# x's halves and the operands of ff2 and w_pe start at another byte within 512 bytes of SBUF

## What is computed

```python
h = rmsnorm(x, norm1_g[i]);  z = h @ w_in[i] + b_in[i]        # 1024 -> 12296 columns
# mLSTM over mq, mk, mv, mo and retention over rq, rk, rv, rg, both chunkwise
merged = sigmoid(gm) * (y_m @ w_bm[i]) + sigmoid(gr) * (y_r @ w_br[i])
x = x + merged @ w_out[i]
h2 = rmsnorm(x, norm2_g[i])
x = x + square(relu(h2 @ w_ff1[i] + b_ff1[i])) @ w_ff2[i] + b_ff2[i]   # 1024 -> 4096 -> 1024
h3 = rmsnorm(x, norm3_g[i])
x = x + sigmoid(h3 @ w_pe_gate[i]) * (p[i] @ w_pe[i])
```

## The kernel before

| buffer | first byte | modulo 512 |
|---|---|---|
| `raw` / `w_lo` | 2176 | 128 |
| `w_hi` | 34944 | 128 |
| `x_hi_lo`: hi half, alias `free_a` | 59520 | 128 |
| `x_hi_lo`: lo half, alias `free_b` | 75904 | 128 |
| `xn` | 108672 | 128 |
| `BIG` / `BIGR` | 179072 | 384 |

## Time and profile before

### The profile page before, as it was taken

How to read it: one execution, slowest core, us unless ns; L and a number is a source line. 1 busy time by engine, 2 the same in 40 slices (tenths; PEclk the granted TensorE clock), 3 DMA queues, 4 the chain that set the end, 5 groups by cost and what they waited for, 6 DMA issues and landing times.

```text
span 2379.8 us, 32080 instructions
## 1 busy us (share of the span) xinstructions
PE 2292.7 (96%) x13686; PEld 1954.9 (82%) x13686; DVE 1496.3 (63%) x1893; ACT 1028.4 (43%) x1256; POOL 0.2 (0%) x4
## 2 busy tenths in 40 slices
PE   6998989999998999999999999999999999999997
PEld 3775667777786878888998878999989987789997
DVE  4777543333346576765877767666678767767475
ACT  4255441121225265544663435444555534435343
POOL 0000000000000000000000000000000000000000
PEclk9999989999998999999999999999999999999999
DMA  8530034444422252555555544454555545345552
GB/s 329 206 148 1 36 126 193 159 195 159 159 106 107 88 125 89 195 188 205 215 185 178 184 171 160 178 191 178 179 188 196 187 176 198 141 178 183 177 183 101
DMA packets 61397, 389.12 MB, mean 164 GB/s; under 512 B 6600, under 2 KB 11080, under 8 KB 16072
## 3 DMA queue, kind: packets, MB, share of 16 engines
q1 hardware_dynamic: 61256, 387.08, 44.7%
HBM read 386.01 MB, written 1.05 MB: 163 GB/s over the span
## 4 chain that ended last, share of the span: by engine, by line
PE 86%; DVE 7%; ACT 4%; issue 2%; DMA 1%; SPq 0%; DVEq 0%; ACTq 0%
PE PS L509 23%; PE PS L511 23%; PE PS L510 23%; PE PS L615 5%; PE PS L613 3%; PE PS L864 1%; DMA raw<-chunks_in 1%; PE PS L1041 1%; DVE w_lo L1722 1%; ACT w_hi L1244 1%; ACT xn L1322 1%; PE PS L743 1%; PE PS L1023 1%; PE PS L703 1%; PE PS L768 1%
## 5 line engine op out<-in xcount | busy, mean ns | idle before, releaser
L1722 DVE TENSOR_TENSOR w_lo<-raw,w_hi 128x2048 fp32r<-128x2048 f32 x300 | 683.4, 2290 | 492.7 <-ACT w_hi L1244 491.6
L1244 ACT ACTIVATE w_hi<-raw 128x2048 fp32r<-128x2048 f32 x300 | 571.6, 1912 | 696.8 <-PE PS L511 323.8
L509 PE MATMUL PS<-x_hi_lo,w_hi 128*128 128x256 f32 (+1 forms) x1760 | 546.2, 310 | 9.7 <-DVE x_hi_lo L1787 5.2
L511 PE MATMUL PS<-x_hi_lo,w_lo 128*128 128x256 f32 (+1 forms) x1760 | 543.4, 309 | 0.0
L510 PE MATMUL PS<-x_hi_lo,w_hi 128*128 128x256 f32 (+1 forms) x1696 | 518.6, 306 | 0.0
L509 PEld LDWEIGHTS PS<-x_hi_lo,w_hi 128*128 128x128 f32 x1760 | 337.1, 192 | 36.3 <-issue 19.6
L511 PEld LDWEIGHTS PS<-x_hi_lo,w_lo 128*128 128x128 f32 x1760 | 337.0, 191 | 16.8
L510 PEld LDWEIGHTS PS<-x_hi_lo,w_hi 128*128 128x128 f32 x1696 | 325.1, 192 | 14.0
L509 PE MATMUL PS<-w_hi,x_hi_lo 128*128 128x512 f32 (+1 forms) x800 | 317.9, 397 | 15.6 <-DVE x_hi_lo L1787 10.8
L510 PE MATMUL PS<-w_lo,x_hi_lo 128*128 128x512 f32 (+1 forms) x800 | 313.5, 392 | 0.0
L511 PE MATMUL PS<-w_hi,x_hi_lo 128*128 128x512 f32 (+1 forms) x800 | 313.5, 392 | 0.0
(11 more groups left out here) (326 smaller groups left out, 2666.1 us busy)
## 6 DMA issues: line engine op xcount, KB each, us to landing
raw<-chunks_in SPq DMA_DIRECT2D x348, 1024.0 KB, 4.8
bias_ring<-brows_in SPq DMA_DIRECT2D x32, 256.0 KB, 5.0
G<-nrows_in SPq DMA_DIRECT2D x2, 1536.0 KB, 6.7
BIG<-rel_in SPq DMA_DIRECT2D x4, 512.0 KB, 7.7
free_b<-rel_in SPq DMA_DIRECT2D x4, 512.0 KB, 7.8
tabt<-tabs_in SPq DMA_DIRECT2D x1, 1536.0 KB, 11.7
X<-x_in SPq DMA_DIRECT2D x1, 1024.0 KB, 8.5
X<-ctx_in SPq DMA_DIRECT2D x1, 1024.0 KB, 10.5
```

Of the source, the lines that this page charges most:

```text
L509: pe.matmul(o, lhs[0], rhs[0], start=start, stop=False, **more)
L511: return pe.matmul(o, lhs[1], rhs[0], start=False, stop=stop, **more)
L1244: act.activation(w_hi[:, i % HI_RING, :], ring[:, n % RING, :], ACT.Copy).then_inc(*hi_ready.now(n))
L1722: dve.tensor_tensor(w_lo[:, c % RING, :], ring[:, c % RING, :], w_hi[:, i % HI_RING, :].bitcast(F32), ALU.subtract).then_inc(*lo_ready.now(c))
```

## The change

The halves of `x_hi_lo` grow from 4096 to 4224 floats (`X_HALF`), and every view of them that the second block uses starts 112 floats (448 bytes) into its half (`X_AT`). Counted from the arena's start, such an operand begins 64 bytes short of a multiple of 512. `ff2T`, `pT2` and `pw` start 48 floats later in BIG (`FF_AT`), which comes to the same place. Everything placed behind x moves up by 1024 bytes. `x_both` keeps its shape and takes the new start; the views of the first block's wider matmuls (`hT[4]`, `y4T`) and its layer 1 output projection (`yT_na`), `ff_both` and w_bm's and w_br's operands stay where they are modulo 512.

In absolute bytes of the partition, as built:

| operand | before, modulo 512 | after, modulo 512 |
|---|---|---|
| x hi and lo, 256 tokens | 128 | 64 |
| ff2T, pT2 | 384 | 64 |
| w_hi, w_lo | 128 | 128 |

```diff
+X_HALF = 4096 + 128
+X_AT = 112
+FF_AT = 48
...
-        xboth_, xhi_at = place("x_hi_lo", 8192, F32R)
-        xhi_, xlo_, xlo_at = xboth_[:, 0:4096], xboth_[:, 4096:8192], xhi_at + 4096
-        free_a, _ = place("free_a", 4096, F32, xhi_at)
-        free_b, _ = place("free_b", 4096, F32, xlo_at)
+        xboth_, xhi_at = place("x_hi_lo", 2 * X_HALF, F32R)
+        xhi_, xlo_, xlo_at = xboth_[:, 0:X_HALF], xboth_[:, X_HALF:2 * X_HALF], xhi_at + X_HALF
+        free_a, _ = place("free_a", X_HALF, F32, xhi_at)
+        free_b, _ = place("free_b", X_HALF, F32, xlo_at)
...
-        hT = {4: pair_of((xhi_, xlo_), 512, KD), 2: pair_of((xhi_, xlo_), 256, KD)}
-        hT_b = pair_of((xhi_[:, 2048:4096], xlo_[:, 2048:4096]), 256, KD)
+        hT = {4: pair_of((xhi_, xlo_), 512, KD), 2: pair_of((xhi_[:, X_AT:], xlo_[:, X_AT:]), 256, KD)}
+        hT_b = pair_of((xhi_[:, X_AT + 2048:], xlo_[:, X_AT + 2048:]), 256, KD)
...
-        mv = free_a[:, 2048:4096].rearrange("p (t c) -> p t c", t=2)
-        mo = free_b[:, 2048:4096].rearrange("p (t c) -> p t c", t=2)
+        mv = free_a[:, X_AT + 2048:X_AT + 4096].rearrange("p (t c) -> p t c", t=2)
+        mo = free_b[:, X_AT + 2048:X_AT + 4096].rearrange("p (t c) -> p t c", t=2)
...
-        hr = [free_a[:, 2048:4096], free_b[:, 2048:4096]]
+        hr = [a[:, X_AT + 2048:X_AT + 4096] for a in (free_a, free_b)]
...
-        x_both = xboth_[:, :].rearrange("p (h k t) -> p h k t", h=2, t=256)[:, :, 0:KD, :]
+        x_both = xboth_[:, :].rearrange("p (h n) -> p h n", h=2)[:, :, X_AT:X_AT + KD * 256].rearrange("p h (k t) -> p h k t", t=256)
...
-        ff2T = pair_of((bigr(0, 4096), bigr(4096, 4096)), 256, 16)
-        pT2 = (bigr(8192, 512), bigr(8704, 512))
-        pw = big(9216, 2048).rearrange("p (k t) -> p k t", k=KD)
+        ff2T = pair_of((bigr(FF_AT, 4096), bigr(FF_AT + 4096, 4096)), 256, 16)
+        pT2 = (bigr(FF_AT + 8192, 512), bigr(FF_AT + 8704, 512))
+        pw = big(FF_AT + 9216, 2048).rearrange("p (k t) -> p k t", k=KD)
```

More of the change, by code:

```diff
@@ L303, in build_program @@
         k_l0, mv_l0 = (G[:, 2048 * i:2048 * i + 2048].rearrange("p (t h d) -> p t h d", t=4, h=4) for i in range(2))
-        y4 = free_b[:, :].rearrange("p (t d) -> p t d", t=4)
+        y4 = free_b[:, 0:4096].rearrange("p (t d) -> p t d", t=4)
         y4T = pair_of((xhi_, xnr_), 512, KD)
@@ L329, in build_program @@
         v["nkT"] = pair_of((xnr_, G_r), 512, 8)
-        v["rel"] = [a.rearrange("p (t h k) -> p t h k", t=2, h=NA_H // 2) for a in (big(2048, 4096), free_b[:, :])]
+        v["rel"] = [a.rearrange("p (t h k) -> p t h k", t=2, h=NA_H // 2) for a in (big(2048, 4096), free_b[:, 0:4096])]
         cond = bias_[:, 544:544 + KD * COND_W].rearrange("p (k c) -> p k c", c=COND_W)
```

## The result

| | before | after |
|---|---|---|
| median | 2385.65 us (6 runs) | 2364.84 us (6 runs) |
| lowest, highest run | 2382.41, 2389.61 | 2359.87, 2377.08 |
| span of the profiled execution | 2379.8 | 2358.1 |

The ratio of after to before is 0.9917 with a 95% interval of 0.99 to 0.9934: 20.8 us or 0.8% faster. The forecast was 2367 us, faster. The span went down by 21.7 us. (The forecast started from the median of the first three runs, 2388.16 us; the six give 2385.65.) One thing was not forecast: the runs of the changed kernel spread over 17 us, those of the kernel before over 7.

What follows compares the result with a forecast made beforehand. TensorE was taken as the bound in the second block. Span 2379.8 - 21.9 - 1.0 = 2356.9, plus some 2 us of gain not passed on, 2359; the median 8.4 us above, 2367 us; 8 in 10 range 2345 to 2400.

Steps and rivals of the forecast that it cites:

- What bounds the kernel: Second block: TensorE busy every microsecond in the first projections, ff1 and ff2, so the start-to-start price of a matmul decides.
- Part 1: Second block, 5472 matmuls of 256 columns with shifted moving operand: 120.0 to 116 ns each, -21.9 us.
- Part 2: Second block's token-major projections, x stationary and w moving, 1536 matmuls at 226.7 ns: 0, bounds -10 to +8 us.
- Part 3: First block's `project_wide` with x, 352 pairs: -1 us taken, +4.7 us if both matmuls lose a third step.
- Part 5: VectorE and ScalarE reading and writing the moved operands: cost doesn't depend on the start, 0.
- Part 6: Second-block streams: splitting and landing of weight chunks stay covered; nine tenths to all of the gain passes, some 2 us lost.
- From span to median: Whole kernel: the runs' median stands 8.4 us above the span, so 2359 us of span becomes 2367 us.
- The reading behind it: Matmul streams: moving operand and next stationary tile collide in SBUF on a 64-byte grid, losing time in 6.7 ns steps.
- a step less in full: Rival for the second block's 256-column matmuls: 113.5 ns each, -36 us, 2352 to 2355 us; chance 0.20 around 2353.
- nothing changes: Rival: the settled 120.0 ns belongs to the two rates, not the start; 2388 us, from 2381 to 2395; chance 0.27.
- The change doesn't do what it says: Rival: if absolute place counts, the new start is 64 past a multiple of 512; counted with "nothing changes".
- Slower: Rival: a step more, +37 us to 2425 at 256 columns, or +8 us to 2396 token-major only; chance 0.23.

Runs made afterwards that it cites:

- e3: The kernel before with w moved up by 64 bytes, x and BIG left modulo 512 (distances -64 and 192); 2378.82 us, ratio 0.9975.
- e4: The changed kernel with each group of four of ff2's operand tiles at a start of its own, 16 distances to w; 2371.41 us, one run.
- e7: The changed kernel unaltered, profiled and timed once more; 2363.13 us, ratio 0.9908.
- e1: The changed kernel with x's views back at their old start, only ff2T, pT2 and pw shifted; 2371.85 us, ratio 0.995.
- e8: The changed kernel with `project_wide`'s x back at distance 0 and `yT_na` moved to -64; 2357.6 us, ratio 0.9883.
- e2: The kernel before with the whole arena shifted by 448 bytes, x and w together; 2381.93 us, one run.
- e10: Built on e8, with hT[2] at 192 bytes above w and hT_b, mv, mo, hr, `yT_na` and BIG at 112; 2358.73 us, ratio 0.9896.
- e9: The changed kernel with x, ff2T and pT2 at 112 bytes above w in place of 64 below; 2363.62 us, ratio 0.9907.
- e11: The changed kernel with ff2T, pT2 and pw back at their old start, only x's views shifted; 2371.76 us, ratio 0.9945.
- the two scans: e4, and the changed kernel with 13 more ff2 distances, x's 256-column views at 16 and some 512-column operands moved; 2371.41 and 2394.19 us.

## Why the prediction was right, point by point

- *What bounds the kernel* held: the stretches of the earlier trace rows are as full as before, and a nanosecond per matmul came through.
- *Part 1, the 256-column matmuls*: the direction was right and the size too small. Taken were 116 ns and -21.9 us; measured are 113.4 (BIG) and 115.3 (x), -31.2 us. The term that was mis-sized is the 116 ns, the choice between the bounds: I leaned to the 117.5 of the earlier trace rows. The bound from the gate product, 113.5, is what most streams have. About 820 of the 5472, w_out2 with the first chunks of ff1 and most of pe_g, sit at 117.8. I had read that 117.5 as a stream not yet settled; e3, e4 and e7 have 117.8 as a rhythm that holds for hundreds of matmuls. Whether the 8 matmuls of the earlier trace rows were that rhythm, left again, no run tells.
- *Part 2, token-major*: 0 was taken with -10 to +8, measured +2.9 us. The sign of the reason was right (the settled state for 512 columns was already the cheap one), the value inside the bounds.
- *Part 3, `project_wide`*: -1 was taken, measured +3.2 us with `ff_both`, inside the bound of +4.7. The sign was wrong. The dear price also occurs with x unshifted (e1, e8), and `ff_both`, which was not moved, has it after the change, so its 0.8 us are not the shift's; that x has it at -64 in all five profiles speaks for the shift in the other 2.4.
- *Part 5, the other engines*: VectorE's splitting takes 2289 ns as before. 0 held.
- *Part 6, what is late next*: 2 us of the gain was not to pass; 2.6 us of longer pauses were measured, among them 0.9 us in which TensorE waits for `w_lo`. The cover held inside the streams and failed by a little at their heads; by the sign that the prediction named, VectorE's `w_lo` as TensorE's releaser in ff1 (0.54 us at 1561.56 us), it failed there.
- *From span to median*: 8.4 us were added as what lies around the span. That was the wrong reading of this number. The profiled run of after took 2359.87 us with a span of 2358.1, so 1.8 us lie around it; the rest is the spread between runs. The medians of six stand 5.9 us above the span before and 6.7 after, which makes 2 us of the error.
- *The reading behind it*, a loss in steps of 6.7 ns on a grid of 64 bytes, did not hold. It said rightly that the relative place matters and that some place is cheaper. But 117.8 at -64, 118.3 at 48 and 123.3 at 4 are no whole steps from 120.0, and starts 4 bytes apart differ (the table of distances).

So the median hides two errors of some 9 us in part 1 and 8 us in parts 2, 3 and 6, which nearly cancel: 2359 of span forecast, 2358.1 measured, for a mixture that wasn't forecast. The direction was earned; that the size came out within 2 us is luck. Summed up as it happened, the rival "a step less in full" (113.5 ns) describes the rows better than the forecast; its 2352 to 2355 us was missed by the streams at 117.8 (820 x 4.5 ns = 3.7 us), the +6.1 us of parts 2 and 3, and the pauses.

The other rivals: *nothing changes* fell with the rows at 1572.56 to 1659.60 us. It rested on the equal 120.0 of x and BIG, at distances 0 and 256, and the table of distances shows why that said nothing: distances 256 bytes apart had one price wherever both were tried. *The change doesn't do what it says*, by the absolute place, fell with e2. *Slower* fell for this distance; its mechanism exists (123.3 ns at a distance of 4, 233.3 token-major at 112). The page "TensorE: Matmul & The Clock Gate" of the Trainium skill (section "Step-by-step: what each phase is for") says that loading the next weights takes no read bandwidth from the running matmul, since each operand has a read port of its own; by that rule the start could not matter. The runs disagree: one form took 113.3 to 123.3 ns, depending on the distance. The same page's N/2.4 + 2.5 ns (section "Back-to-back issue gap"), 109.2 ns here, is given there for an isolated matmul gap without weight loads. No stream reached it; the lowest is 113.3.

What causes the loss is still argued, not shown. The runs show that it depends on the distance between the two operands in SBUF, equal wherever two distances 256 bytes apart were tried, on the width of the moving one, and on the rhythm a stream has fallen into. Two reads that meet in the same part of SBUF could do all three; no run looked inside.

## What to carry to other kernels

Where TensorE is busy without a gap and matmuls of one form stand in long streams, read the distance from start to start: part of what it has above columns / 2.4 GHz (6.7 of 13.3 ns here) can be placed away, by moving the moving operand relative to the stationary one and keeping every view of a buffer at one place modulo 256 bytes. Scan the distance in one run, by giving neighbouring tiles different starts, and for each width and role apart: the best for 256 columns moving (112, -64) cost the 512-column streams up to 6.7 ns. Then time it in several runs and profile it twice, because a place with two rhythms (16 worst, -64 somewhat, 112 in no long stream of 256 columns) can have another price in the next execution.

## What was new about the hardware

- The price of a 256-column float32r matmul in a stream lay between 113.3 and 123.3 ns over the distances tried, and 4 bytes matter: 120.0, 123.3 and 117.3 at 0, 4 and 12.
- One distance can have several self-holding prices: 113.3 and 117.8 at -64; 113.3, 116.7 and 118.7 at 16; 228.9 and 233.3 for the token-major streams with x at -64; 346.7 and 353 ns per pair for `project_wide` at 0. Which one a stream takes can differ between executions of one program (e7). That this widens the spread of a kernel's times is not shown: it was 17 us after the change but 10 in its repeat, 5 in e8 and e10, 4 in e9 and 7 before, on four to six runs each, and between the profiles of after and e7 the first block differs more (2.3 us, by the granted clock) than the second (1.5).
- A switch from one moving buffer to another needs no pause to bring the other price (e1, e11), while a stream of one moving buffer without a gap over 130 ns between two starts kept its price from its thirteenth matmul to its end: so it is in the second block of the ten profiles other than the two scans and e9, in each of some 300 such streams of 40 to 432 matmuls. In e9 one gap of 130 ns was followed by nine distances of 116 to 121 ns, and then by 113.3 again.
